# Last attention: one PSUM bank for the compressed steps, output rows beside eighteen heads, turned weights moved by VectorE alone

## The reference, cut to what matters

```
q = rmsnorm(q_raw) * hd**-0.5                       # 12 heads of 64, in 2 groups
kc, vc = compress(...)                              # gelu(flat @ w1) @ w2, 15 compressed rows
p_c = masked_softmax(q @ kc + bias_c);  o_c = p_c @ vc
p_s = masked_softmax(q @ k_sel + bias_s); o_s = p_s @ v_sel
p_w = masked_softmax(q @ k_w + bias_w);   o_w = p_w @ v_w
y_tok = g0 * o_c + g1 * o_s + g2 * o_w
y_mem = softmax(q_mem @ mem_k) @ mem_v              # 4 heads
x = x + concat([y_tok, y_mem]) @ w_out
```

## Time and profile before

| | us |
|---|---|
| median of 3 executions | 1539.57 (1536.43 to 1539.68) |
| profiled execution, its own time | 1537.14 |
| its span in the trace | 1535.4 |
| PE busy | 1438.6 (94%) |
| DVE busy | 887.0 (58%) |
| ACT busy | 684.2 (45%) |
| mean granted clock of TensorE | 0.953 of full speed |

### The profile page before, as it was taken

One profiled execution on the slowest core, in us unless ns is written; L12 is line 12 of the kernel. 1 busy time (PEld: TensorE's weight loads), 2 busy tenths in 40 slices (PEclk: granted clock), 3 DMA queues, 4 the chain that ended last, 5 costly groups with the idle time before them and its releaser, 6 DMA issues.

```text
span 1535.4 us, 24444 instructions
## 1 busy us (share of the span) xinstructions
PE 1438.6 (94%) x10298; PEld 1353.5 (88%) x10298; DVE 887.0 (58%) x1183; ACT 684.2 (45%) x985; POOL 182.1 (12%) x174
## 2 busy tenths in 40 slices
PE   7998999999799899999998959899999889899998
PEld 6997999999799799999986748899998778799997
DVE  6476655456546766555567563645547765474554
ACT  5544543435435345443456332444346543354442
POOL 2002210101200112100022100211112300010000
PEclk9999999999999999999999977899999977899999
DMA  8631365554463135765544431354554430245552
GB/s 228 188 110 55 111 194 191 192 167 149 123 180 110 56 110 190 236 199 179 192 125 150 164 110 49 111 198 165 185 200 137 139 117 1 71 137 188 182 191 83
DMA packets 159657, 225.10 MB, mean 147 GB/s; under 512 B 19081, under 2 KB 127625, under 8 KB 159548
## 3 DMA queue, kind: packets, MB, share of 16 engines
q1 hardware_dynamic: 159548, 223.55, 45.2%
HBM read 222.44 MB, written 1.09 MB: 146 GB/s over the span
## 4 chain that ended last, share of the span: by engine, by line
PE 83%; DVE 9%; issue 3%; ACT 3%; POOL 1%; DMA 0%; DVEq 0%; SPq 0%; ACTq 0%; POOLq 0%
PE ps L2338 17%; PE ps L2340 16%; PE ps L2339 16%; PE ps L2330 5%; PE ps L2331 4%; PE ps L2332 4%; PE ps L2617 2%; DVE xT L1425 2%; PE ps L2618 2%; PE ps L2619 2%; DVE w_lo L1401 2%; PE ps L2969 2%; ACT w_hi L797 2%; DVE h L1440 1%; PE ps L2851 1%
## 5 line engine op out<-in xcount | busy, mean ns | idle before, releaser
L1401 DVE TENSOR_TENSOR w_lo<-raw,w_hi 128x2048 fp32r<-128x2048 f32 (+4 forms) x209 | 478.5, 2294 | 286.5 <-ACT w_hi L797 284.0
L2338 PE MATMUL ps<-xT,w_hi 128*128 128x256 f32 x1600 | 462.6, 289 | 13.4 <-DVE w_lo L1401 6.9
L797 ACT ACTIVATE w_hi<-raw 128x2048 fp32r<-128x2048 f32 (+4 forms) x209 | 392.2, 1879 | 168.9 <-PE ps L2340 81.5
L2339 PE MATMUL ps<-xT,w_hi 128*128 128x256 f32 x1600 | 456.9, 286 | 0.0
L2340 PE MATMUL ps<-xT,w_lo 128*128 128x256 f32 x1600 | 456.8, 286 | 0.0
L2338 PEld LDWEIGHTS ps<-xT,w_hi 128*128 128x128 f32 x1600 | 311.4, 195 | 17.5 <-DVE w_lo L1401 13.5
L2339 PEld LDWEIGHTS ps<-xT,w_hi 128*128 128x128 f32 x1600 | 311.5, 195 | 0.5
L2340 PEld LDWEIGHTS ps<-xT,w_lo 128*128 128x128 f32 x1600 | 311.2, 194 | 0.0
L2338 PE MATMUL ps<-hT,w_hi 128*128 128x256 f32 x640 | 182.7, 286 | 5.4 <-DVE hT L1887 4.6
L2339 PE MATMUL ps<-hT,w_hi 128*128 128x256 f32 x640 | 182.1, 285 | 0.0
L2340 PE MATMUL ps<-hT,w_lo 128*128 128x256 f32 x640 | 182.0, 284 | 0.0
(11 more groups left out here) (330 smaller groups left out, 2072.5 us busy)
## 6 DMA issues: line engine op xcount, KB each, us to landing
raw<-in_w_up_dram SPq DMA_DIRECT2D x54, 1024.0 KB, 5.4
raw<-in_w_down_dram SPq DMA_DIRECT2D x54, 1024.0 KB, 5.0
raw<-in_w_gate_dram SPq DMA_DIRECT2D x22, 1024.0 KB, 5.4
raw<-in_w_in_dram SPq DMA_DIRECT2D x14, 1024.0 KB, 5.5
raw<-in_a_w_in_dram SPq DMA_DIRECT2D x10, 1024.0 KB, 5.6
raw<-in_w_o_dram SPq DMA_DIRECT2D x8, 1024.0 KB, 5.0
raw<-in_w_ple_gate_dram SPq DMA_DIRECT2D x8, 1024.0 KB, 5.0
raw<-in_w_out_dram SPq DMA_DIRECT2D x8, 1024.0 KB, 4.9
```

The lines of the kernel that those rows point to most:

```text
L797: nc.scalar.activation(w_hi[:, p % RH, 0:piece_width(p)], raw[:, p % RR, 0:piece_width(p)], ACT.Copy).then_inc(E["hi_ready"], 1)
L1401: nc.vector.tensor_tensor(w_lo[:, p % RH, 0:w], raw[:, p % RR, 0:w], w_hi[:, p % RH, 0:w].bitcast(F32), ALU.subtract).then_inc(E["lo_ready ...
L2338: nc.tensor.matmul(out_, w[0][:, kk, c], x(0, k), start=start and j == 0, stop=False, skip_group_check=True)
L2339: nc.tensor.matmul(out_, w[0][:, kk, c], x(1, k), start=False, stop=False, skip_group_check=True)
```

## The change

It does six things, all in the last layer.

1. All compressed steps from the gelu on write to `PS[1]`, the hidden rows to `PS[4]` and `PS[6]`. `PS[4]` to `PS[7]` are then free for the output rows from head 10 on. The steps and the turned pairs now take turns in `PS[1]`: the pair 6 moves from head 12 to head 6, the two transposes and the three outputs of the compressed branch to heads 16, 17 and 18, 20, 21.
2. `ROWS_2` is 10, and the first 40 units stand beside eighteen heads (one to four each); the last 8 stand behind the last head, before and behind the last turned pair.
3. The hidden units are turned first (30 x 512 become 128 x 120), and the gelu works on the turned ones; it stands one head later.
4. VectorE moves the turned weights of all heads.
5. The splits of five pieces move: the first of the `cmp` pieces from ahead of head 0 to head 1 (`ahead_=False`), the next from head 1 to head 2, and the second and third output piece from heads 6 and 7 to heads 12 and 18. The fourth goes from head 22 to head 20.
6. The order of `compressed_out` and `group` at the counts is adapted.

```diff
-        hfun = tflat[0:NSA_G * NCMP, 768:768 + 2 * CMP_HID].rearrange("p (w n) -> p w n", w=2)
+        hfun, hgel = tflat[:, 768:768 + 120], tflat[:, 896:896 + 120]
-        ROWS_2 = 20
-        BESIDE_2 = ((0, 0, 6), (0, 6, 11), (0, 11, 16), (1, 0, 6), (1, 6, 11), (1, 11, 16), (2, 0, 8), (2, 8, 16))
+        ROWS_2 = 10
+        BESIDE_2 = ((0, 0, 2), (0, 2, 4), (0, 4, 6), (0, 6, 8), (0, 8, 10), (0, 10, 11), (0, 11, 12), (0, 12, 13), (0, 13, 14),
+                    (0, 14, 16), (1, 0, 4), (1, 4, 7), (1, 7, 10), (1, 10, 13), (1, 13, 16), (2, 0, 3), (2, 3, 6), (2, 6, 8))
-        GROUP_OUT = (1, 2, 3, 4, 8, 9, 10)
-        COMP_OUT = (5, 6, 7)
+        GROUP_OUT = (1, 2, 3, 4, 6, 9, 10)
+        COMP_OUT = (5, 7, 8)
...
# ScalarE and VectorE
-                wide_evac(("q", 0), 512, z1[:, :, 0:512], ("mix", 1))
+                wide_evac(("q", 0), 512, z1[:, :, 0:512], ("mix", 1), ahead_=False)
...
# ScalarE
-                    if i % 2 and i > MEM_H:
-                        move_pT(i)
...
                     if i == 1:
-                        used(("q", 1), 0)
+                        used(("q", 0), 1)
                     if i == 2:
                         evac_units(query_units(0))
+                        used(("q", 1), 0)
...
                     if i == 6:
                         evac_units(query_units(1))
-                        used(("cmp", 1), 0)
+                        rounded_pair(6)
                     if i == 7:
                         hidden_units(1)
-                        used(("cmp", 1), 1)
                     if i == 8:
+                        act.wait_ge(E["zeroed"], 1)
+                        act.wait_ge(E["gel_t"], 1)
+                        nc.scalar.activation(hfun, PS[1][:, 0:120], ACT.Square).then_inc(E["gel_sq"], 1)
...
                     if i == 12:
-                        rounded_pair(6)
+                        used(("cmp", 1), 0)
...
+                    if i == 18:
+                        used(("cmp", 1), 1)
...
# VectorE
-                    if i % 2 == 0 or i < MEM_H:
-                        move_pT(i)
+                    move_pT(i)
...
-                    if i == 7:
-                        dve.wait_ge(E["gel_sq"], 2)
-                        link(nc.vector.scalar_tensor_tensor(hfun, hfun, 1 / 0.044715, act_hid[0:NSA_G * NCMP, :, :],
-                                                            op0=ALU.add, op1=ALU.mult))
+                        rest_pair(6)
+                    if i == 8:
+                        dve.wait_ge(E["gel_sq"], 1)
+                        link(nc.vector.scalar_tensor_tensor(hfun, hfun, 1 / 0.044715, PS[1][:, 0:120], op0=ALU.add, op1=ALU.mult))
...
-                    if i in (17, 18, 19):
-                        compressed_out(4 * (i - 17))
+                    if i in (18, 20, 21):
+                        compressed_out({18: 0, 20: 4, 21: 8}[i])
+                    if i == 18:
+                        used(("cmp", 1), 1)
                     if i == 19:
                         rest_pair(0)
+                    if i == 20:
+                        used(("w_out", 1), 0)
                     if i == 22:
                         rest_pair(2)
-                        used(("w_out", 1), 0)
...
# TensorE
-                    if i in (12, 19, 22):
-                        pe.wait_ge(E["o_evac"], G0 + {12: 1, 19: COMP_OUT[0], 22: GROUP_OUT[4]}[i])
+                    if i in (6, 19, 22):
+                        pe.wait_ge(E["o_evac"], G0 + {6: GROUP_OUT[0], 19: COMP_OUT[0], 22: COMP_OUT[2]}[i])
...
                 values(NL - 1)
+                out_rows(2, 8, 12)
                 pe.wait_ge(E["o_evac"], G0 + 10)
                 turned_pair(4)
+                out_rows(2, 12, 2 * KD)
```

More of the change, by code:

```diff
@@ L1033, in evac_units, with wide_evac @@
                     n["T"] += 1
-            def wide_evac(stage, width, dst, factor, after_=lambda: None):
+            def wide_evac(stage, width, dst, factor, after_=lambda: None, ahead_=True):
                 p = FIRST[stage]
@@ L1052, in wide_evac @@
                         after_()
-                    split_upto(last + RH)
+                    if ahead_:
+                        split_upto(last + RH)
                     p = last
@@ L1326, in last_heads @@
                                              ).then_inc(E["ce_done"], 1)
[L1327 to L1331 removed]
+                    if i in (16, 17):
+                        t = i - 16
+                        act.wait_ge(E["ct_done"], t + 1)
+                        nc.scalar.activation(PTc[:, 384 * t:384 * t + 384], PS[1][:, 0:384], ACT.Copy).then_inc(E["cte_a"], 1)
+                    if i == 18:
+                        used(("cmp", 1), 1)
                     if i == 19:
                         rounded_pair(0)
+                    if i == 20:
+                        used(("w_out", 1), 0)
                     if i == 22:
                         rounded_pair(2)
[L1336 removed]
                     if i == 25:
@@ L2948, in hidden_rows, with units_turned @@
                     i.then_inc(E["piece_used"], 1)
-                def gelu_turned(w):
-                    for j in range(2):
-                        c = 256 + 32 * j
-                        i = nc.tensor.transpose(PS[(1, 6)[w]][:, c:c + 30], act_hid[0:30, w, P * j:P * j + P],
-                                                ident[0:30, 0:30])
+                def units_turned():
+                    for w in range(2):
+                        for j in range(2):
+                            c = 60 * w + 30 * j
+                            i = nc.tensor.transpose(PS[1][:, c:c + 30], act_hid[0:30, w, P * j:P * j + P], ident[0:30, 0:30])
                     i.then_inc(E["gel_t"], 1)
@@ L3045, in compressed @@
                                 c = (t * NSA_H + a) * 16
-                                m = nc.tensor.matmul(PS[4][:, c:c + 32], q8[:, a // 2, t * P:t * P + P],
+                                m = nc.tensor.matmul(PS[1][:, c:c + 32], q8[:, a // 2, t * P:t * P + P],
                                                      kcT[:, a // HPG, :, :], start=True, stop=True)
                         m.then_inc(E["cs_done"], 1)
-                    if i == 16:
-                        pe.wait_ge(E["ce_done"], 1)
-                        pc = tflat[:, 0:768]
-                        for t in range(NT):
-                            for a in range(3):
-                                c = t * 384 + a * P
-                                m = nc.tensor.transpose(PS[5 + t][:, a * P:a * P + P], pc[:, c:c + P], ident)
-                            m.then_inc(E["ct_done"], 1)
-                    if i in (17, 18, 19):
-                        a = 4 * (i - 17)
+                    if i in (16, 17):
+                        t = i - 16
+                        if t == 0:
+                            pe.wait_ge(E["ce_done"], 1)
+                        else:
+                            pe.wait_ge(E["cte_a"], 1)
+                        pc = tflat[:, 0:768]
+                        for a in range(3):
+                            c = t * 384 + a * P
+                            m = nc.tensor.transpose(PS[1][:, a * P:a * P + P], pc[:, c:c + P], ident)
+                        m.then_inc(E["ct_done"], 1)
+                    if i in (18, 20, 21):
+                        a = {18: 0, 20: 4, 21: 8}[i]
                         if a == 0:
```

82 lines of the change are left out of this document (33 added, 49 removed).

## The result

| | before | after |
|---|---|---|
| median (us) | 1538.78 (1536.43 to 1539.68, 4 runs) | 1528.09 (1527.45 to 1529.15, 4 runs) |
| profiled execution, its span | 1537.14, 1535.4 | 1527.45, 1525.7 |
| PE, DVE, ACT busy | 1438.6, 887.0, 684.2 | 1433.5, 888.7, 679.3 |
| mean granted clock | 0.953 | 0.961 |

What follows compares the result with a forecast made beforehand. PE, busy 94% of the span, was taken to bound the kernel, through waits and half clock. Terms of -23.8 us, cut to -20 for handing over, gave a forecast median of 1518.5 us; 8-in-10 range 1512 to 1531.

Steps and rivals of the forecast that it cites:

- Heads 0 to 3: Last attention's start: moved splits cut the 3.75 us wait to 0.6 and remove the half clock; 6.0 us less counted.
- Heads 4 to 9: Splits leave heads 6 and 7, gelu shrinks; scores(9) to scores(11) takes 5.0 us for 12.7; 7.1 us less.
- Heads 10 to 17: scores(11) to scores(18): 36.0 us at half clock becomes 26.1 with added rows and VectorE waits; 9.9 us less.
- Heads 18 to 27: scores(18) to last values: 7.9 us less from units gone, 6.6 more from waits for VectorE; 1.3 us less.
- The tail: Last values to last piece's first block: chain gets 0.5 us longer, 9.2 us for 8.7; half clock after it stays.
- The sum: Terms total -23.8 us; 3.6 us taken off for handing over between engines leaves -20; forecast median 1518.5 us.
- rival (a): Clock falls for a while in the light heads; 8 to 12 us at half clock cost 4 to 6: 1523.5; chance 0.20.
- Rival (d): VectorE bounds heads 10 to 27, its waits twice those counted, 10 us more: 1528.5 us; chance 0.16.
- (b): Clock falls at head 8 or 9 until the dense rows of head 20: about 1540 us, no change; chance 0.05.
- (c): Clock isn't back by scores(22) either, because units are thin: 18 us more, 1555 us; chance 0.03.
- (e): Rows come early but splits late, so PE waits for w_lo; no size given; chance 0.01.
- The rule of the Trainium skill: A transpose doesn't count as PE being busy in the same way, so light heads 8 and 9 endanger the clock.

Runs made afterwards that it cites:

- the fastest kernel: Changed kernel with second-piece split at head 11, compressed outputs before turned weights, last pair's rest before next split, fourth split at heads 22/23: 1501.45 us, ratio 0.9759.
- the last experiment: The fastest kernel with the two first splits put back ahead of heads 0 and 1: 1512.63 us, ratio 0.9842 to the kernel before.
- the kernel with six units: Changed kernel with second and third splits back at heads 6 and 7, plus six row units together at head 11: 1524.55 us, ratio 0.9912.

## Why the prediction was right, and where it was wrong

**Heads 0 to 3**: right. The wait is 0.73 us where 0.6 was forecast, there is no fall, and up to scores(9) 4.5 us are gone for 5.4. But what the step is worth in the whole kernel varies: alone it gave 1.6 us, and taken out of the fastest kernel it cost 11.2, of which 6.2 are a fall at head 14 that may not be its doing.

**Heads 4 to 9**: right. It is 4.7 us from scores(9) to scores(11) for 5.0, the reciprocal takes 0.90 us for 0.8 to 0.95, and the clock is full; the wait is 0.19 us where I took 0.4 to 0.9. The kernel with the splits back at heads 6 and 7 shows how much hangs on moving these two: without that, 2 us of gain are left, with the rows beside eighteen heads all the same.

**Heads 10 to 17**: the step that failed. It says "18.0 at full" and puts nothing on the clock, though it places 2.2 us of idle PE ahead of values(12). The wait came as worked out (2.14), the clock fell, and 26.1 us became 34.9. The experiment with the split at head 11 shows it: wait and fall went together, and the stretch took 23.4 us. With the wait of 2.1 us that is 25.5, near the 26.1; the other 9.4 us are the clock.

**Heads 18 to 27**: the same. The waits are 1.56 and 2.83 us for 1.5 and 2.7, and at head 22 0.28 for 1.4. Without the 5.1 us of the fall the stretch would be 2.7 us shorter than before, where I had 1.3. With the compressed output first the fall is gone and so are 4.6 us.

**The tail**: right in its size (9.2 us) and its chain. The prediction says that before, PE is at 2.4 GHz behind 1289.5 us; it is at half clock again from 1333.8 to 1344.0, as the tail's last sentence there allows, and most of that is idle time. What I missed is that the split has no need to stand ahead of the pair's rest; 4.7 us lay there (3.6 in the kernel before).

**The sum**: the terms give -23.8 us with a full clock; measured it is -9.8, and without the 15.3 us of the two falls it would be -25.1. So the 3.6 us for handing over that I took off were not needed, and their place was taken by 15.3 us of clock that I gave only a chance of 0.20. (The forecast is also 1 us below its own working: 1517.1 for the profiled execution and 2.4 more for the median are 1519.5, not 1518.5.)

**The rivals**: this was rival (a), by the mechanism it names ("the idle 2.2 us at head 13 is as long as the 2.31 us ahead of the fall"), but twice, so 15 us for its 4 to 6. Its argument against, that 525 to 545 us held 1.00 with PE 13% idle, doesn't carry over: the longest idle time there is 0.88 us. Rival (d) fell, since the waits for VectorE were those counted. Rivals (b) and (c) fell for this kernel by the full clock at scores(11), and (e) since no wait of PE in the last attention ends with `w_lo`.

**Right by the range, not by the account**: the prediction names as a sign of being wrong that "PE's clock is at 0.50 anywhere between", and it was, for 30.7 us. The measured 1528.1 us are almost the 1528.5 of rival (d), whose cause wasn't there, and not the 1523.5 of (a). That the time still lies in the range is in part luck: the range was wide enough for (d).

**The rule of the Trainium skill** (TensorE: Matmul & The Clock Gate, Part 4: PE-mode transpose) was the reason to name the light heads 8 and 9 as a danger. They ran at 1.00 here. In the last experiment the clock fell without a wait during matmuls of 32 columns, not during transposes; in the kernel with six units it fell during the transposes of head 14. No run here isolates the transposes.

**What stays open.** First, when the clock falls. The waits of 2.14 us (three kernels) and of 2.21 us (one) at head 12 had a fall at their end, all seven waits of 2.83 us at head 21 had one, from 1.7 us ahead of their end to 1.5 us behind it, and the eight of 1.56 us at head 19 had none. But at head 22 a wait of 2.06 us had none and one of 1.59 us had one, and waits of 0.99 and 0.84 us at heads 7 and 8 were followed by one in both kernels that have them. Three kernels fell at head 14 with no wait over 0.25 us near, and two didn't; one of the three and the fastest are the same program up to head 20, so the instructions alone don't decide.

Second, when it comes back. Behind the same wait of 2.83 us it was down for 3.4 us in three kernels, and for 6.8, 10.3, 13.7 and 20.5 us in one each. Wherever it fell at heads 7 to 14, it came back (for the second time in the kernel with six units) within 0.6 us of the start of scores(18), in before and in ten others; in the kernel with the first splits alone it was a head later. Why isn't known.

## What to carry to other kernels

When a sum already places a wait of 2 us in one piece where the clock has fallen behind such waits before, put a price for the clock on it, and a wide one: in the kernels with the rows beside heads it was down for 3.4 to 20.5 us behind waits of 2.1 to 2.8 us, which is 2 to 10 us of time. Better still, move what causes the wait to where its engine idles: that cost nothing here and gave 11.4 us. A gain ahead of a stretch at half clock may be eaten by it, so edits are judged together, not one by one. And since the length of a fall varies in kernels that are alike up to there, a difference of a few us between two kernels that both fall isn't yet the worth of an edit.

## What the runs showed of the hardware

- TensorE stayed at 1.2 GHz for 44.3 us in which it was busy for 43.95, with scores, transposes, values and one or two units of rows a head. With six units in a row in that program (4.1 us) it was back at 2.4 GHz 0.6 us behind them, 28 us earlier.
- It also fell from 2.4 to 1.2 GHz with no idle time over 0.25 us near, in three kernels: during 24 matmuls of 32 columns at head 14, or 0.5 us behind them. In two kernels it passed them at 2.4 GHz.
- Behind the same wait the length at half clock differed: 10.3 and 20.5 us in two kernels that are alike up to there. Some kernels with falls spread widely in time (1518.87 to 1528.63 us), others don't (after, 1527.45 to 1529.15); the kernel with no fall spreads over 2.7 us.
- VectorE's reciprocal took 0.90 us on 120 columns (128 partitions) where 512 columns (30 partitions) took 3.34: 7.5 and 6.5 ns a column.
